# A weight remainder shared between VectorE and GpSimd in a fused two-block transformer kernel

## The reference

```
for l in range(2):                                     # first block
    proj = x @ w_in[l]                                 # 1024 -> q,k,v (twice), latents, 3 gates
    na   = neighbourhood_attention(q, k, v, bias)      # 8 heads of 64
    df   = diff_attention(q, k, v)                     # softmax 1 - lambda * softmax 2, 4 heads
    ml   = latent_attention(c_q, c_kv, k_rope, w_qb, w_kvb)   # 8 heads of 64 + 32 rotated
    merged = sum(sigmoid(gate_i) * (branch_i @ w_branch[i]))
    x = layer_norm(alpha * x + merged @ w_out[l])
    x = layer_norm(alpha * x + (silu(x @ g) * (x @ u)) @ w_ffn_out[l])
for l in range(2):                                     # second block
    x = x + concat(gqa_attention, spatial_gating) @ w_o[l]
    x = x + (silu(gate) * up) @ w_down[l]              # gate, up = depthwise_conv(h @ w_up)
```

## Time and profile before

| | us |
|---|---|
| median of three runs | 1531.62 |
| the profiled execution | 1531.43 |
| its span | 1530.0 |
| TensorE busy in the span | 1471.4 (96%) |
| VectorE | 1006.3 (66%) |
| ScalarE | 788.9 (52%) |
| GpSimd | 68.3 (4%) |

### The profile page before, as it was taken

One profiled execution on the slowest core, in us unless ns is written; L12 is line 12 of the kernel. 1 busy time (PEld: TensorE's weight loads), 2 busy tenths in 40 slices (PEclk: granted clock), 3 DMA queues, 4 the chain that ended last, 5 costly groups with the idle time before them and its releaser, 6 DMA issues.

```text
span 1530.0 us, 18329 instructions
## 1 busy us (share of the span) xinstructions
PE 1471.4 (96%) x7161; PEld 1204.7 (79%) x7161; DVE 1006.3 (66%) x1349; ACT 788.9 (52%) x1122; POOL 68.3 (4%) x100
## 2 busy tenths in 40 slices
PE   5999999899999999999999999999999999999998
PEld 4788787778887787787778887777888877778887
DVE  5565885765547655785774555877777767767675
ACT  3564654344343555655343443675655657765663
POOL 1000000000001000000010000210000011000000
PEclk9999999999999999999999999999999999999999
DMA  9544653566564544552666565436465544445551
GB/s 312 178 146 136 210 174 100 190 194 202 186 214 141 209 140 143 179 164 85 192 218 192 168 202 180 131 101 206 151 201 175 188 142 163 141 158 197 166 176 72
DMA packets 167317, 260.99 MB, mean 171 GB/s; under 512 B 8768, under 2 KB 106720, under 8 KB 166720
## 3 DMA queue, kind: packets, MB, share of 16 engines
q1 hardware_dynamic: 166048, 252.03, 50.8%
q0 software_dynamic: 896, 6.74, 1.2%
q10 hardware_dynamic: 288, 1.05, 0.2%
HBM read 258.74 MB, written 1.05 MB: 170 GB/s over the span
## 4 chain that ended last, share of the span: by engine, by line
PE 85%; DVE 8%; ACT 4%; issue 2%; POOL 1%; DMA 1%; SPq 0%; ACTq 0%; DVEq 0%
PE ps L382 14%; PE ps L386 14%; PE ps L384 14%; PE ps L455 11%; PE ps L457 11%; PE ps L456 11%; DVE wlo L1444 2%; PE ps L522 1%; PE ps L966 1%; ACT whi L1023 1%; PE ps L532 1%; PE ps L509 1%; PE ps L703 1%; DVE proj L2008 1%; PE ps L412 1%
## 5 line engine op out<-in xcount | busy, mean ns | idle before, releaser
L1444 DVE TENSOR_TENSOR wlo<-raw,whi 128x2048 fp32r<-128x2048 f32 (+1 forms) x238 | 528.6, 2230 | 280.4 <-ACT whi L1023 280.1
L1023 ACT ACTIVATE whi<-raw 128x2048 fp32r<-128x2048 f32 (+1 forms) x238 | 441.6, 1866 | 210.0 <-PE ps L386 112.1
L382 PE MATMUL ps<-whi,xTh 128*128 128x512 f32 x704 | 278.1, 395 | 6.1 <-DVE wlo L1444 2.4
L386 PE MATMUL ps<-whi,xTl 128*128 128x512 f32 x704 | 274.7, 390 | 0.0
L384 PE MATMUL ps<-wlo,xTh 128*128 128x512 f32 x704 | 274.5, 390 | 0.0
L455 PE MATMUL ps<-whi,xTh 128*128 128x512 f32 (+3 forms) x640 | 253.4, 396 | 9.9 <-DVE xTl L1470 3.2
L457 PE MATMUL ps<-whi,xTl 128*128 128x512 f32 (+3 forms) x640 | 244.6, 382 | 0.0
L456 PE MATMUL ps<-wlo,xTh 128*128 128x512 f32 (+3 forms) x640 | 243.9, 381 | 0.0
L382 PEld LDWEIGHTS ps<-whi,xTh 128*128 128x128 f32 x704 | 132.3, 188 | 35.1 <-DVE wlo L1444 3.2
L386 PEld LDWEIGHTS ps<-whi,xTl 128*128 128x128 f32 x704 | 132.2, 188 | 27.9
L384 PEld LDWEIGHTS ps<-wlo,xTh 128*128 128x128 f32 x704 | 132.4, 188 | 26.3
(11 more groups left out here) (184 smaller groups left out, 1632.8 us busy)
## 6 DMA issues: line engine op xcount, KB each, us to landing
raw<-in_w_in SPq DMA_DIRECT2D x124, 512.0 KB, 4.6
raw<-in_w_ffn_in SPq DMA_DIRECT2D x88, 512.0 KB, 4.9
raw<-in_w_up SPq DMA_DIRECT2D x88, 512.0 KB, 4.9
raw<-in_w_ffn_out SPq DMA_DIRECT2D x44, 512.0 KB, 4.5
raw<-in_w_down SPq DMA_DIRECT2D x44, 512.0 KB, 4.7
raw<-in_w_branch SPq DMA_DIRECT2D x24, 512.0 KB, 4.6
raw<-in_w_out SPq DMA_DIRECT2D x16, 512.0 KB, 4.4
raw<-in_w_o SPq DMA_DIRECT2D x16, 512.0 KB, 4.7
```

The costliest lines, as they stand in the source:

```text
L382: PE.matmul(o, ah, hi[:, j, b], start=first and kt == 0, stop=False)
L386: mm = PE.matmul(o, al, hi[:, j, b], start=False, stop=last and j == c - 1 and i == len(kts) - 1)
L1023: AC.activation(m.whi[:, i % SPLIT, 0:w], m.raw[:, slot, 0:w], ACT.Copy).then_inc(s.w_hi, 1)
L1444: DV.tensor_tensor(m.wlo[:, i % SPLIT, 0:w], m.raw[:, slot, 0:w], m.whi[:, i % SPLIT, 0:w].bitcast(F32), ALU.subtract).then_inc(s.w_lo, 1)
```

## The change

Of the first block's pieces d, lq, lkv, g, q, kv, b and the third of n, and of the second block's u, s and a, those with an odd number have their remainder made by GpSimd, which counts them on a semaphore of its own, `w_lo_pool`. TensorE and SyncE wait on the one or the other, each with the count of the pieces of its own engine (`remainder_there`). That is 40 pieces: 32 of 2048 columns, two of 1536, four of 1152 and two of 1024. GpSimd's program gets calls of its own `split_to` between the inverse roots, and the root of the differential heads is moved behind the load of the next bias table. On VectorE, `split_to` skips those pieces; several catches of the attention stages get `ahead=0` with the remainders done at the next catch; the latent rotation moves from the eviction of the first branch product to the last group of the differential stage; and in stage "w" the remainders are done one by one between the merged sums and the low parts. One catch of ScalarE's is split in the same way.

```diff
+def on_pool(name):
+    return name[2] in (("d", "lq", "lkv", "g", "q", "kv", "b"), ("u", "s", "a"))[name[0] - 1] or name[2:] == ("n", 2)
+def remainder_there(k, i):
+    return (k.s.w_lo_pool if k.own[i] else k.s.w_lo), sum(o == k.own[i] for o in k.own[:i + 1])
@@ build
+        own += [on_pool(name) and i % 2 == 1 for i in range(first[name], after[name])]
@@ sync_program, tensor_program
-            SP.wait_ge(s.w_lo, i - RING + 1)
+            SP.wait_ge(*remainder_there(k, i - RING))
-                    PE.wait_ge(s.w_lo, i0 + i + 1)
+                    PE.wait_ge(*remainder_there(k, i0 + i))
@@ pool_program
+    def split_to(pieces):
+        while n["split"] < pieces:
+            i = n.up("split") - 1
+            if not k.own[i]:
+                continue
+            slot, w = i % RING, k.size[i]
+            PO.wait_ge(s.w_hi, i + 1)
+            PO.tensor_tensor(m.wlo[:, i % SPLIT, 0:w], m.raw[:, slot, 0:w], m.whi[:, i % SPLIT, 0:w].bitcast(F32),
+                             ALU.subtract).then_inc(s.w_lo_pool, 1)
...
+        split_to(k.first[1, L, "d", 2])
         rsqrt(s.moments, *rows(24, 2), 1.0 / MLA_Q, RMS_EPS)
+        split_to(k.first[1, L, "g", 0, 0])
         rsqrt(s.moments, *rows(26, 2), 1.0 / MLA_KV, RMS_EPS)
-        rsqrt(s.moments, *rows(16, 8), 1.0 / P, RMS_EPS)
         if L + 1 < DEPTH:
             PO.wait_ge(s.negm, 24 * L + 8)
             load_bias(L + 1)
+        split_to(k.first[1, L, "b", 1, 0])
+        rsqrt(s.moments, *rows(16, 8), 1.0 / P, RMS_EPS)
+        split_to(k.first[1, L, "w", 0])
...
         rsqrt(s.qk_sq, *rows(32, 16), 1.0, 64 * RMS_EPS, out=s.qk_root)
+        split_to(k.first[2, L, "s", 0])
         rsqrt(s.vv_sq, *rows(8, 16), 1.0 / 64, RMS_EPS, out=s.vv_root)
+        split_to(k.first[2, L, "a", 0])
         rsqrt(s.out_sq, *rows(26, 2), 1.0 / 512, RMS_EPS, out=s.out_root)
+        split_to(k.first[2, L, "up", 0])
@@ scalar_program, differential stage
+            split_to(k.seen[1, L, "df", g, 2][0] + SPLIT)
             catch(1, L, "df", g, 3)
@@ vector_program
+            if k.own[i]:
+                continue
-            if (i, j) == (0, 0):
-                rotate_latent(L, th)
...
-            catch(1, L, "na", g, 1)
+            catch(1, L, "na", g, 1, ahead=0 if g else SPLIT)
...
-            catch(1, L, "df", g, 1)
-            catch(1, L, "df", g, 2)
+            if g == 4:
+                for part in range(2):
+                    rotate_latent(L, part)
+            catch(1, L, "df", g, 1, ahead=0 if g else SPLIT)
+            catch(1, L, "df", g, 2, ahead=0 if g else SPLIT)
+            split_to(k.seen[1, L, "df", g, 2][0] + SPLIT)
             catch(1, L, "df", g, 3, ahead=SPLIT - 1)
...
-            catch(1, L, "ml", g, 1)
+            catch(1, L, "ml", g, 1, ahead=0 if g else SPLIT)
...
-        catch(1, L, "w", 0)
-        catch(1, L, "w", 1)
+        w0 = k.first[1, L, "w", 0]
+        catch(1, L, "w", 0, ahead=0)
+        split_to(w0 + 1)
+        catch(1, L, "w", 1, ahead=0)
         turn_lo_quarter(0, 0, 0.5)
-        catch(1, L, "w", 2)
-        for th, n4 in ((1, 0), (0, 1), (1, 1)):
-            turn_lo_quarter(th, n4, 0.5)
+        catch(1, L, "w", 2, ahead=0)
+        turn_lo_quarter(1, 0, 0.5)
+        turn_lo_quarter(0, 1, 0.5)
+        split_to(w0 + 2)
+        turn_lo_quarter(1, 1, 0.5)
         catch(1, L, "w", 3)
```

More of the change, by code:

```diff
@@ L49 @@
     "raw0", "raw1", "raw2",
-    "w_hi", "w_lo", "w_used",
+    "w_hi", "w_lo", "w_lo_pool", "w_used",
     "th0_sum",
@@ L69 @@
 Tensors = namedtuple("Tensors", [n for n, _, _ in SBUF] + ["ps", "down", "cw", "sgw", "brow"])
-Kernel = namedtuple("Kernel", "nc t out m s raws free size first after call bank halves seen")
+Kernel = namedtuple("Kernel", "nc t out m s raws free size first after call own bank halves seen")
 class Count(defaultdict):
@@ L121, in build @@
 def build(nc, t, out):
-    first, after, call, size = {}, {}, {}, []
+    first, after, call, size, own = {}, {}, {}, [], []
     for name, pieces in gemm_names():
@@ L134, in build @@
         s = Sems(*[ctx.enter_context(nc.semaphore(name)) for name in SEMS])
-        k = Kernel(nc, t, out, m, s, (s.raw0, s.raw1, s.raw2), (s.free0, s.free1, s.free2), size, first, after, call,
+        k = Kernel(nc, t, out, m, s, (s.raw0, s.raw1, s.raw2), (s.free0, s.free1, s.free2), size, first, after, call, own,
                    {}, [], {})
```

## The result

The changed kernel took 1577.41 us (median of six runs, 1575.33 to 1578.35) beside 1531.62 for the kernel before: ratio 1.0296, 95% interval 1.0282 to 1.0309. The prediction was 1551, with a range of 1533 to 1565. The direction was right, the size was not: of 45.8 us it had 19.7. One execution of the run z2 took 2989.89 us, the other three 1551.86 to 1553.93; nothing on record says why, and its ratio is that of the three.

A forecast was written before the change was run, and what follows sets the result against it. TensorE, busy 96% of the span, was taken to bound the kernel. Output product 11.2, rotation 4.2, elsewhere 4.3 and differential stage 0 sum to 19.7 us on 1531.43: 1551, range 1533 to 1565.

The forecast's parts named there:

- order of the output product: Merge and output product: early merge gains nothing (+0.2), slow clock +1.6, remainder 40 late +3.8; 5.6 a layer, 11.2 us.
- rotation of block two: Second block: GpSimd's remainder stops VectorE's rotation up to 4.2 us against 2.1 slack; +2.1 in each layer, 4.2 us.
- GpSimd's disturbance elsewhere: Softmax chains outside the rotation: GpSimd's remainders stop VectorE's work; +4.3 us, bounds 0 and 8.7.
- attention orders (differential stage): Differential stage: at most 6.9 us of waits go, but stops replace them; taken as 0, bounds -6.9 and +3.
- nine places: Softmax stops at piece 15 (1.4 us) and others (0.8 to 1.3 each): some 8.7 us, half taken.
- wait behind at most one: GpSimd's short root operations wait behind at most one remainder; no cost was added for it.
- The clock: Output product: lower clock after the first wait costs 1.6 us a layer; also after the second only in the bound.
- the bound of 14.4: Output product, both layers: upper bound if the second wait lowers the clock as well.
- The price of a remainder: A 2048-column remainder on GpSimd takes 4.2 us, bounds 2.28 and 10.1.
- Rival (c): A GpSimd remainder takes 10.1 us, so rotation and softmax stops cost more: 1590 us, chance 0.05.
- (a): GpSimd and VectorE hardly disturb each other; only the output product costs, the differential stage gains: 1536 us, chance 0.22.
- (b): Faster: remainder 40 doesn't hold TensorE, targeted waits (12.0 us) and slow clock (1.6 a layer) go: 1516 us, chance 0.08.

The follow-up runs named there:

- z2: The changed kernel, forty remainders on GpSimd, with y3's better order of the output product on VectorE and ScalarE: 1553.56 us (ratio 1.0136).
- x1: The kernel before with only VectorE's new order in the merge and output product, no piece on GpSimd: 1547.72 us (ratio 1.0108).
- x3: The changed kernel with all 238 remainders on VectorE, every reordering kept: 1542.94 us (ratio 1.0070 to the kernel before).
- x2: The changed kernel with VectorE's old order in the merge and output product: 1558.86 us (ratio 1.0178 to the kernel before).
- x4: The kernel before, its orders on VectorE and ScalarE kept, with only the forty remainders moved to GpSimd: 1566.64 us (ratio 1.0228).
- y4: x2 with the second block's six pieces back on VectorE, thirty-four left on GpSimd: 1550.31 us (ratio 1.0124 to the kernel before).
- u1: The changed kernel with VectorE's scaling of two maxima rewritten to take its second input from PSUM: 1565.12 us (ratio 1.0217 to the kernel before).
- y1: The kernel before, no remainder moved, with four unused 512-column subtractions on GpSimd whenever it would take a piece: 1568.08 us (ratio 1.0236).
- y3: x3 with VectorE taking remainders 39 to 41 before the eviction, and ScalarE three quarters' high parts before piece 41's rounding: 1517.49 us (ratio 0.9907).
- z4: The kernel before with y3's two edits to the output product's order alone: 1524.31 us (ratio 0.9951).
- y2: The changed kernel with GpSimd's forty subtractions replaced by writes of zeros: 1540.97 us (ratio 1.0062 to the kernel before).

## Why the prediction was wrong

| term | predicted | measured |
|---|---|---|
| order of the output product | +11.2 | +15.9 (x1) |
| rotation of block two | +4.2 | +4.8 (two steps of the lag, at line 869) |
| GpSimd's disturbance elsewhere | +4.3 | +27 |
| attention orders (differential stage) | 0 | -4.8 (x3 against x1) |
| sum | 19.7 | 43, and 45.8 in all |

The 27 is worked out: x2 less what before would take with the attention orders alone (1531.6 - 4.8 = 1526.8) is 32.1; less the rotation's 4.8. The terms miss the whole by 2.6, the difference between x2's 18.5 and x1's 15.9 for the order, which the medians can't resolve.

**The step that failed** is "with the first that is nine places, some 8.7 us; since earlier shifts move several of them off their collision, I take half, 4.3 us". Its mechanism was right, its list and its halving were not. The term was 4.3 and measured 27. The list names eight places, not nine (pieces 15, 9, 30, 31, 35, 99 and 157 in both layers), and one of them, piece 30, has an even number and stays on VectorE. Matmul by matmul between x3 and the changed kernel, the lag rises by 0.5 us or more at twenty places, by 26.1 us together, 4.8 of them the rotation's; the rest of the 32.6 us that this lag ends at is in smaller steps, slow matmuls behind waits among them. The steps at the seven named places that exist come to about 9 us (1.95 at piece 15, 2.47 at 99, 1.43 at the second 157): the sum before the halving, 8.7, was right for them. So the halving took away 4, and some 18 lay at places that the list did not have, 5.4 of them in the differential stage (0.9, 1.3 and 3.2 at pieces 25, 27 and 101), which the prediction netted in another term.

The halving had the reason that shifts break collisions up. They did not: in the changed kernel, x2, x4, y4, z2 and u1, whose orders and lags differ, the same seven scalings of rows stand, for the same 4.5, 1.6, 1.5, 3.9, 1.7, 4.5 and 2.4 us, to 0.05. The likely reason, which no run tests, is that GpSimd's operations follow ScalarE's rounding, which follows the same TensorE progress as VectorE's softmax work, so both shift together.

The list had the scaling of rows, 1.14 us of work. It did not have the scaling of maxima, 0.17 us of work, which u1 shows to be worth 12.3 us: I looked for stops where VectorE had much to do, and should have looked for what waits behind whatever stands. Nor did it have GpSimd's inverse root: "wait behind at most one" remainder was put at nothing, and its two waits make steps of 1.36 and 0.51 us.

**The differential stage** was netted: gain against stops, "I take 0". Apart, the gain is real and at its ceiling: x3's lag falls by 1.55 and 2.04 us at two places of this stage, in each layer, 7.2 in all against 6.9 in the earlier trace rows. Some 4.5 are left at the end, as 0.4 us a layer is lost before the merge and x3's output product costs 9.3 and 9.5 us where x1's costs 8.5. The stops were part of the 27, outside the bound of +3: at 639 and 651 two pieces stop the maxima for 3.85 and 3.41 us, and the row at 657.37 is waited for 3.23 us.

**The output product** went as described, step by step: remainder 40 behind the eviction and the statistics, 3.79 us waited (3.8 predicted), a wait of 5.41 before it ("one of nearly 5"), the merged sum earlier to no avail (+0.4 us at the transposes of 276.88 in layer 0 and 0.2 in layer 1, 0.2 predicted). The clock was mis-sized. I charged 1.6 us for the first wait and left the second to the bound. Behind the first wait seven to nine matmuls follow each other at 0.43 us instead of 0.23, behind the second twelve to thirteen: 1.5 and 2.5 us in layer 0, 1.9 and 2.7 in layer 1. In x1, where GpSimd is not involved, the stage comes to 8.5 us a layer instead of 5.6, and even the bound of 14.4 for both layers was too low.

**The price of a remainder** on GpSimd was right: 4.2 taken, 4.58 undisturbed (103.30) and 4.83 in the mean of 32:

```profile
L299 POOL TENSOR_TENSOR wlo<-raw,whi 128x2048 fp32r<-128x2048 f32 x32 | 154.5, 4827 | 189.7 <-ACT whi L1052 189.7
```

The Trainium skill's 4.5 us ("GPSIMD Engine Reference", section 3.1, "Elementwise — side-by-side cycle accounting") agrees with it. Rival (c), 1590 us, was 13 too high where the forecast was 26 too low, but its condition is false: pieces take 4.8 us, not 10.1.

**The rotation** was right: TensorE's wait in front of the first transpose made a step of 2.41 us in layer 0 and 2.39 in layer 1, where 2.1 was predicted. But the second block costs 8.5 us in all (y4). Of the other 5 us of the lag between y4 and x2, 1.4 are a step at the probabilities' transposes in layer 0, 1.5 slow matmuls behind the rotation in layer 1, and 1.5 two steps at the end of that stage.

**Rivals.** (a) is refuted by y1 and x4, (b) by x1: the merged sum came 3.2 us earlier, but remainder 39 took that back and remainder 40 cost 4 us more. Its condition, "remainder 40 is there when the first half ends", was met by y3, and there the time is 1517.5, next to the 1516 that the rival gave. That is near by luck in part, since y3 shares nothing with GpSimd, while the rival's sum was for the forty pieces moved.

## What to carry to other kernels

An idle engine isn't free help if it reads the memory that a busy one reads: count each operation moved to GpSimd as a stop of up to its whole length (4.8 us here) for what VectorE does then, except the operations that the rows show to run on beside it (here those with an input in PSUM and the reciprocals), and look first for the shortest operations on the critical chain, since a stop doesn't scale with them. Don't halve a list of collisions because shifts will break them up, when both engines are paced by the same third one. When a wait is removed by moving work later, follow the moved work to its next reader on each engine; here the same idea with a few lines in another order is 7.7 us faster alone (z4) instead of 15.9 slower (x1).

## What the hardware showed that I had not expected

- An operation of VectorE's with one tensor input can stand too. The 128x2 scaling went from 0.17 us to as much as 4.2, while the reciprocal, also from SBUF to SBUF, kept its 167 ns, ten times in the midst of a remainder of GpSimd's. Operations with an input in PSUM (the memory of TensorE's sums) kept their times as well: the same scaling with its second input in PSUM took 157 ns in u1. The Trainium skill, page "SBUF — State Buffer", section "Who interferes with whom", frees operations with one input from SBUF only under a condition: `tensor_scalar` can run in a mode that uses both pairs of ports, and then contends with GpSimd, while two-input operations contend only with its reads. The runs agree in what they can show: y2's writes left the two-input remainders at 2288 ns and stretched the scalings to 398 and 267 ns in the mean (349 and 169 in x3). No row names the mode, but in x3 operations of this kind take 348 ns for 256 columns and 416 for 384 (line 1618), about 0.5 ns a column, where two-input operations take 0.42 us for 256 and 0.69 for 512, about 1.0.
- Cutting GpSimd's operation in four doesn't shorten the stop of a run of short operations (38.2 us instead of 35.8 for the 64 rows), and makes GpSimd itself slower, 6.1 us a piece.
- Waits of 5.41 and 3.79 us were followed by 3 and 5 us of matmuls at the lower clock; one of 0.54 us was not (1.00 throughout). The lower level's matmuls follow each other at 0.43 us, the higher level's at 0.23, near the factor of two between the levels of 1.2 and 2.4 GHz.
